# Gate-and-up products: one matmul over both activation parts, with GpSimd folding the halves

## The reference

```
def swiglu(x, w_gu, w_down):
    g, u = jnp.split(x @ w_gu, 2, axis=-1)     # x 512x1024, w_gu 1024x5632
    return (jax.nn.silu(g) * u) @ w_down
```

## Time and profile before

| | us |
|---|---|
| median of 3 runs (lowest, highest) | 2150.84 (2150.32, 2151.48) |
| the profiled execution's own time | 2148.99 |
| its span | 2147.3 |
| TensorE busy | 2129.5 |
| VectorE busy | 1612.1 |
| ScalarE busy | 1195.5 |
| GpSimd busy | 110.4 |

### The profile page before, as it was taken

The page is one execution under the profiler, slowest core; times in us unless marked ns, Lnnn a source line. Parts: engine busy times, 40 slices in busy tenths (PEclk is TensorE's granted clock), DMA queues, the critical chain, the costliest instruction groups (busy, mean ns, idle before and its releaser), DMA issues.

```text
span 2147.3 us, 36470 instructions
## 1 busy us (share of the span) xinstructions
PE 2129.5 (99%) x13624; PEld 1916.4 (89%) x13624; DVE 1612.1 (75%) x2299; ACT 1195.5 (56%) x1943; POOL 110.4 (5%) x104
## 2 busy tenths in 40 slices
PE   9999999999999999999999999999999999999998
PEld 8999988775888899998899998898889889999987
DVE  8888886798565688889688889855367566888894
ACT  6555654476564565556465556455456446555562
POOL 0000000576000000000000000000000000000000
PEclk9999999999999999999999999999999999999999
DMA  4333432221352223333413333322323422333332
GB/s 158 107 98 115 139 115 68 79 77 52 137 168 79 79 99 107 98 117 118 157 62 105 107 114 131 127 84 94 104 79 118 157 79 72 105 106 100 129 107 97
DMA packets 74498, 227.80 MB, mean 106 GB/s; under 512 B 8177, under 2 KB 22641, under 8 KB 74402
## 3 DMA queue, kind: packets, MB, share of 16 engines
q1 hardware_dynamic: 69936, 214.98, 30.3%
q10 hardware_dynamic: 4466, 11.53, 1.5%
HBM read 224.39 MB, written 2.10 MB: 105 GB/s over the span
## 4 chain that ended last, share of the span: by engine, by line
PE 93%; DVE 4%; ACT 1%; POOL 1%; issue 1%; DMA 0%; DVEq 0%; POOLq 0%; ACTq 0%
PE ps L2411 13%; PE ps L2413 13%; PE ps L2412 13%; PE ps L2457 7%; PE ps L2458 7%; PE ps L2459 7%; PE ps L511 6%; PE ps L512 6%; PE ps L513 6%; PE ps L2583 4%; PE ps L2584 4%; PE ps L2585 4%; PE ps L2347 1%; DVE e_sc L2071 0%; DVE e_max L2070 0%
## 5 line engine op out<-in xcount | busy, mean ns | idle before, releaser
L2411 PE MATMUL ps<-t_hi,w_hi 128*128 128x256 f32 x1280 | 362.3, 283 | 0.0
L2412 PE MATMUL ps<-t_lo,w_hi 128*128 128x256 f32 x1280 | 362.2, 283 | 0.0
L2413 PE MATMUL ps<-t_hi,w_lo 128*128 128x256 f32 x1280 | 362.2, 283 | 0.0
L449 DVE TENSOR_TENSOR w_lo<-w_raw,w_hi 128x1024 fp32r<-128x1024 f32 x180 | 222.6, 1240 | 172.2 <-ACT w_hi L444 171.5
L444 ACT ACTIVATE w_hi<-w_raw 128x1024 fp32r<-128x1024 f32 x186 | 195.9, 1056 | 169.5 <-DMA w_raw<-in_wstream 117.3
L1684 DVE TENSOR_TENSOR w_lo<-f,w_hi 128x1024 fp32r<-128x1024 f32 x152 | 186.2, 1225 | 123.9 <-ACT w_hi L956 123.9
L2411 PE MATMUL ps<-x_hi,w_hi 128*128 128x256 f32 x960 | 271.7, 283 | 0.0
L2412 PE MATMUL ps<-x_lo,w_hi 128*128 128x256 f32 x960 | 271.7, 283 | 0.0
L2413 PE MATMUL ps<-x_hi,w_lo 128*128 128x256 f32 x960 | 271.7, 283 | 0.0
L511 PE MATMUL ps<-x_hi,w_hi 128*128 128x256 f32 (+1 forms) x736 | 250.3, 340 | 1.9 <-DVE x_lo L1561 1.1
L512 PE MATMUL ps<-x_lo,w_hi 128*128 128x256 f32 (+1 forms) x736 | 245.9, 334 | 0.0
(11 more groups left out here) (390 smaller groups left out, 4642.6 us busy)
## 6 DMA issues: line engine op xcount, KB each, us to landing
w_raw<-in_wstream SPq DMA_DIRECT2D x286, 512.0 KB, 3.5
w_raw_odd<-in_wstream SPq DMA_DIRECT2D x80, 512.0 KB, 3.5
x_raw<-in_wstream SPq DMA_DIRECT2D x28, 512.0 KB, 5.8
gain_bc<-in_wstream SPq DMA_DIRECT2D x8, 512.0 KB, 7.0
tmp<-in_post_gains ACTq DMA_DIRECT2D x8, 512.0 KB, 3.6
gain_bc<-in_gains ACTq DMA_DIRECT2D x7, 512.0 KB, 4.7
h<-in_x SPq DMA_DIRECT2D x4, 512.0 KB, 6.1
c_mem<-in_mem ACTq DMA_DIRECT2D x2, 1024.0 KB, 5.4
```

Of the source, the lines that this page charges most:

```text
L449: nc.vector.tensor_tensor(wl, raw(v), wh.bitcast(f32), ALU.subtract).then_inc(w_ready, 1)
L2411: nc.tensor.matmul(dst, wh[:, at], xh[:, b, :], start=first, stop=False, skip_group_check=True)
L2412: nc.tensor.matmul(dst, wh[:, at], xl[:, b, :], start=False, stop=False, skip_group_check=True)
L2413: last = nc.tensor.matmul(dst, wl[:, at], xh[:, b, :], start=False, stop=final, skip_group_check=True)
```

## The change

In `product` one matmul of 512 columns takes the upper weights by both activation parts (upper and lower, now neighbours in one tile `x_both` or `t_both`), into the two halves of a bank; a matmul of 256 columns adds the lower weights by the upper activations to the first half. What a bank holds is then the sum of its two halves, and the copies and gate sums work on 512 columns:

```
-                    xh, xl = moving(MOVING[n])
+                    both = moving(MOVING[n])
                     for b in range(KT // 2):
                         at = slice(b * P, (b + 1) * P)
-                        first, final = start and b == 0, b == KT // 2 - 1
-                        nc.tensor.matmul(dst, wh[:, at], xh[:, b, :], start=first, stop=False, skip_group_check=True)
-                        nc.tensor.matmul(dst, wh[:, at], xl[:, b, :], start=False, stop=False, skip_group_check=True)
-                        last = nc.tensor.matmul(dst, wl[:, at], xh[:, b, :], start=False, stop=final,
-                                                skip_group_check=True)
+                        nc.tensor.matmul(dst, wh[:, at], both[:, :, b, :], start=start and b == 0, stop=False,
+                                         skip_group_check=True)
+                        last = nc.tensor.matmul(dst[:, 0, :], wl[:, at], both[:, 0, b, :], start=False,
+                                                stop=b == KT // 2 - 1, skip_group_check=True)
```

ScalarE copies whole banks (K1, K2, K3, K5 are 512 wide); the silu waits for the new gate fold and stands behind `last_upper`:

```
                     else:
+                        act.wait_ge(gu_free, n0 + PLAIN + 2)
                         act.wait_ge(u_sum, pair_count(it, par, 1, s0 + 2))
-                    nc.scalar.activation(place, bank(SETS[par][src])[:, 0:HB], ACT.Copy).then_inc(kept, 1)
+                    nc.scalar.activation(place, bank(SETS[par][src]), ACT.Copy).then_inc(kept, 1)
 def pair_silu(it, par):
-                    act.wait_ge(g_sum, pair_count(it, par, 2, 2 * s0 + 4))
+                    act.wait_ge(g_fold, pair_count(it, par, 1, s0 + 1))
...
                     sum_upper(*nxt, 1)
-                    pair_silu(it, par)
                     act.wait_ge(w_free, pair_count(it, par, 2, u0 + 4))
                     last_upper(1 - par)
+                    pair_silu(it, par)
```

GpSimd takes over `up_second` (512 columns, then its own fold), folds the gate and writes the last lower weights:

```
+                def up_second(it, par):
+                    pool.wait_ge(kept, pair_count(it, par, 4, 4 * s0 + 4))
+                    nc.gpsimd.tensor_tensor(K5, K5, K3, ALU.add).then_inc(u_add, 1)
+                    pool.wait_ge(u_add, pair_count(it, par, 1, s0 + 1))
+                    k5 = tmp[:, 0:1, :]
+                    nc.gpsimd.tensor_tensor(act_tile(it, par)[:, 1:2, :], k5[:, :, 0:HB], k5[:, :, HB:SEQ], ALU.add)\
+                        .then_inc(u_sum, 1)
+                def gate_fold(it, par):
+                    pool.wait_ge(g_sum, pair_count(it, par, 2, 2 * s0 + 4))
+                    nc.gpsimd.tensor_tensor(g_both, g_both, g_rest, ALU.add).then_inc(g_fold, 1)
+                def last_lower(it, par):
+                    pool.wait_ge(w_hi_ready, pair_count(it, par, 2, u0 + 2))
+                    pool.wait_ge(w_ready, pair_count(it, par, 2, u0 + 1))
+                    wh, wl = half_slots(i, 6, 1)
+                    nc.gpsimd.tensor_tensor(wl, pair_raw(par)[:, SEQ:UW], wh.bitcast(f32), ALU.subtract)\
+                        .then_inc(w_ready, 1)
+                def period(it, par, more=True):
+                    up_second(it, par)
+                    gate_fold(it, par)
+                    if more:
+                        last_lower(it + par, 1 - par)
```

VectorE loses `up_second` and `last_lower`; its gate sums are 512 wide and go to `g_parts`; the up half that lies in bank a is folded by a reduction out of PSUM, and one product of 512 columns replaces two:

```
                 def plain_lower(it, par):
                     dve.wait_ge(w_hi_ready, pair_count(it, par, 2, u0 + 1))
+                    dve.wait_ge(w_ready, pair_count(it, par, 2, u0))
...
+                    dve.wait_ge(gu_free, pair_count(it, par, 1, n0 + 2))
+                    nc.vector.tensor_tensor(g_parts[:, 0, :], bank(SETS[par][2]), K1, ALU.add).then_inc(g_sum, 1)
...
+                def up_first(it, par):
+                    dve.wait_ge(w_free, pair_count(it, par, 2, u0 + 4))
+                    b = SETS[par][0]
+                    nc.vector.tensor_reduce(act_tile(it, par)[:, 0, :], bank(b).rearrange("p (a c) -> p c a", a=2),
+                                            AX.X, ALU.add).then_inc(u_first, 1)
+                def pair_product(it, par):
+                    up_first(it, par)
+                    pair_mul(it, par)
...
+                    nc.vector.tensor_tensor(tile, tile, g_both, ALU.mult).then_inc(gu_free, 1)
```

More of the change, by code:

```diff
@@ L105, in trunk @@
         with ExitStack() as early:
-            x_raw = [early.enter_context(nc.sbuf_tensor("x_raw0", [P, KT, SEQ], f32))]
-        x_hi = sb("x_hi", [P, KT, SEQ], f32r)
+            x_raw = [early.enter_context(nc.sbuf_tensor(f"x_raw{n}", [P, KT, SEQ], f32)) for n in range(2)]
         with ExitStack() as early:
+            early.enter_context(nc.sbuf_tensor("x_upper", [P, KT, SEQ], f32r))
             w_late_x = early.enter_context(nc.sbuf_tensor("w_late_x", [P, 2, UW], f32r))
-        with ExitStack() as early:
-            x_raw += [early.enter_context(nc.sbuf_tensor("x_raw1", [P, KT, SEQ], f32))]
-        x_lo = sb("x_lo", [P, KT, SEQ], f32r)
+        x_both = sb("x_both", [P, 2, KT, SEQ], f32r)
+        x_hi, x_lo = x_both[:, 0, :, :], x_both[:, 1, :, :]
         w_raw = sb("w_raw", [P, 2, UW])
@@ L129, in part_sb @@
                 return own.enter_context(nc.sbuf_tensor(name, shape, dt))
-            part_sb("act_first", [P, 2, SEQ])
-            t_hi = part_sb("t_hi", [P, 4, KT // 2, SEQ // 2], f32r)
-            t_lo = part_sb("t_lo", [P, 4, KT // 2, SEQ // 2], f32r)
+            g_parts = part_sb("g_parts", [P, 2, SEQ])
+            t_both = part_sb("t_both", [P, 2, 4, KT // 2, SEQ // 2], f32r)
+            t_hi, t_lo = t_both[:, 0, :, :, :], t_both[:, 1, :, :, :]
             w_raw_odd = part_sb("w_raw_odd", [P, 2, UW])
@@ L247, in trunk @@
         g_sum = sem("g_sum")
+        g_fold = sem("g_fold")
+        u_add = sem("u_add")
+        u_first = sem("u_first")
         u_sum = sem("u_sum")
@@ L459, in moving @@
             if n >= T1:
-                return t_hi[:, n - T1, :, :], t_lo[:, n - T1, :, :]
+                return t_both[:, :, n - T1, :, :]
             blocks = slice(0, KT // 2) if n == B11 else slice(KT // 2, KT)
             tokens = slice(HB, SEQ) if n == B22 else slice(0, HB)
-            return x_hi[:, blocks, tokens], x_lo[:, blocks, tokens]
+            return x_both[:, :, blocks, tokens]
         def half_slots(i, first, n):
@@ L503, in pair_in, with act_tile @@
             return it * 16 + (RAW_COUNT[u] - PLAIN // 2) * 16
-        g_both, u_second = tmp[:, 0, :], tmp[:, 1, 0:HB]
-        K1, K2, K5, K3 = (tmp[:, 2 + n // 2, n % 2 * HB:(n % 2 + 1) * HB] for n in range(4))
+        halves_of_g = g_parts[:, :, :].rearrange("p t (a b) -> p t a b", a=2)
+        g_both, g_rest = halves_of_g[:, :, 0, :], halves_of_g[:, :, 1, :]
+        K5, K3, K1, K2 = (tmp[:, n, :] for n in range(4))
+        def act_tile(it, par):
+            if isinstance(it, int):
+                return act_raw[:, 2 * it + par:2 * it + par + 1, :].rearrange("p o (a b) -> p (o a) b", a=2)
+            return act_raw[:, bass.ds(2 * it + par, 1), :].rearrange("p o (a b) -> p (o a) b", a=2)
         SEVENS = [nffn[i] * SEVEN - PLAIN for i in range(NP)]
@@ L766, in even, with ffn @@
                 poly(3)
+            def ffn(i):
+                s0, u0 = SEVENS[i], U[i, "gate_up"]
+                def up_second(it, par):
[19 more added lines that the diff above has]
+                        last_lower(it + par, 1 - par)
+                with pool.Fori(PLAIN // 2, FT // 2 - 1) as it:
+                    period(it, 0)
+                    period(it, 1)
+                period(FT // 2 - 1, 0)
+                period(FT // 2 - 1, 1, False)
             def gla(i):
@@ L783, in _ @@
                     pool.wait_ge(h_ready, TT * i)
-                if parts[i][0] == "even":
+                if parts[i][0] == "ffn":
+                    ffn(i)
+                elif parts[i][0] == "even":
                     even(i)
@@ L1695, in gate_first @@
                     dve.wait_ge(w_free, pair_count(it, par, 2, u0 + 3))
-                    nc.vector.tensor_tensor(g_both[:, 0:HB], bank(SETS[par][2])[:, 0:HB], K1, ALU.add).then_inc(g_sum, 1)
+                    dve.wait_ge(gu_free, pair_count(it, par, 1, n0 + 2))
+                    nc.vector.tensor_tensor(g_parts[:, 0, :], bank(SETS[par][2]), K1, ALU.add).then_inc(g_sum, 1)
                 def gate_second(it, par):
                     dve.wait_ge(prod, pair_count(it, par, 5, 5 * s0 + 5))
[L1700 to L1705, removed]
+                    nc.vector.tensor_tensor(g_parts[:, 1, :], bank(SETS[par][1]), K2, ALU.add).then_inc(g_sum, 1)
+                def up_first(it, par):
[6 more added lines that the diff above has]
+                    pair_mul(it, par)
                 def pair_mul(it, par):
@@ L1709, in pair_mul @@
                     dve.wait_ge(u_sum, pair_count(it, par, 1, s0 + 3))
[L1710 to L1718, removed]
+                    dve.wait_ge(u_first, pair_count(it, par, 1, s0 + 1))
+                    tile = act_tile(it, par)
+                    nc.vector.tensor_tensor(tile, tile, g_both, ALU.mult).then_inc(gu_free, 1)
                 def period(it, par, front):
@@ L1728, in period @@
```

(15 more changed lines are left out.)

## The result

Forecast: 2243 us, within 2165 to 2280, slower. Measured: the changed kernel takes 2274.02 us (median of 4 runs, 2273.10 to 2275.48), the kernel before 2150.74 (4 runs beside them, 2150.32 to 2151.48). The ratio is 1.0574, with a 95% interval of 1.0561 to 1.0586: 5.7% slower. The profiled execution took 2273.49 us, its span is 2271.8.

The account below looks back on a forecast made before the run. It took a chain through ScalarE, GpSimd and VectorE to bound the kernel: 9.7 + 19 x 11.24 us per FFN against 201.6, +23.1 x 4 = +92 on 2149.0, plus 1.8 for the runs' median: 2243 us, range 2165 to 2280.

Parts of the forecast that it names:

- The order that decides: In each pair, copy K3, GpSimd's up operations, gate fold, silu, K1 in turn: TensorE waits 1.5 us before product three.
- K1: ScalarE's copy out of PSUM for the next pair, made after this pair's silu; product three waits for it; end at 7.02.
- hand-overs at the port: GpSimd and VectorE SBUF reads exclude each other; whoever comes second waits; three such hand-overs in the chain of a pair.
- 0.15 us of overlap: Time by which a held SBUF operation overlaps the one before; without it the chain is 0.45 us longer, the total 34.
- What TensorE gains: Gate-and-up products: a block of three matmuls becomes two, 0.347 instead of 0.360 us; 29.9 us gained in all.
- both port cases: The forecast, with SBUF reads held as in the rows (chance 0.62), and the rival of half the port cost (0.15).
- No cover lost: Rival: GpSimd's and VectorE's fp32 operations pass each other at the port, chain 5.5 us, total 2121 us; chance 0.09.
- The port costs half: Rival: GpSimd needs 30% less or passes the second sum_lower; period 10.3 us, total 2172 us; chance 0.15.
- Longer GpSimd work: Rival: GpSimd's half-row folds cost 10% more or the small one 1.29 us; period 11.7, total 2277 us; chance 0.12.
- The wide matmul brings nothing: Rival: the moving operand's two halves cost what they save; 2256 us, inside the forecast's own range, no separate chance given.
- load of the shared reads: Per pair, VectorE's two-SBUF-input operations 6.0 us plus GpSimd's 4.0 make 10.0, over the 9.71 that TensorE allows.
- K3: ScalarE's copy out of PSUM after product five, forecast to end at 0.88 us; GpSimd's up sum waits for it.

Follow-up runs that it names:

- TensorE's part alone: The kernel before with only the matmuls changed, copies and gate sums still 256 wide, GpSimd idle: 2135.74 us, ratio 0.9928.
- `sum_lower` out of PSUM: The changed kernel with VectorE's two sum_lower subtractions taking their first operand from a PSUM bank instead of SBUF: 2164.64 us, ratio 1.0061 to the kernel before.

## Why the prediction was right, and what it mis-sized
**The order that decides: right, in place and size.** Counted from the start of product six (114.93), the ends of the steps in the pair above against the prediction's, in us:

| end of | predicted | measured |
|---|---|---|
| GpSimd up sum | 2.87 | 2.83 |
| gate_second | 2.41 | 2.30 |
| second sum_lower | 3.99 | 3.94 |
| half fold | 4.6 | 4.53 |
| gate fold | 5.85 | 5.78 |
| silu | 6.50 | 6.44 |
| K1 | 7.02 | 6.93 |
| start of product three | 7.06 | 6.98 |

Over 68 middle pairs the median start of product three is 7.04. So the hand-overs at the port, read from three overlaps of the earlier trace rows, hold for the new operations as well. The 0.15 us of overlap also hold: the second `sum_lower` ends at 118.87, the half fold 0.59 later, where one alone takes 0.74. The signs that it named came: 76 waits before product three, 105 us (forecast about 100); GpSimd's up sum at 1850 ns, well above 1.29 (`sum_lower`, at 1255 against 1.22, was held in the first period of an FFN alone, 2.32 us there); ScalarE waiting for the gate fold in every pair; GpSimd busy 584 us.

**What TensorE gains: the term that was mis-sized.** The prediction took the wide step from down's 0.227, among matmuls of one width. Here it is 0.234 to 0.237 and a block 0.3537 us: 28 x 80 x 0.0063 = 14 us instead of 30, as TensorE's part alone measured (15). In the stalled loop only products three to five count. They take 4.34 us (median; 114.93 - 110.58 = 4.35 above) instead of 4.16: 12 x 0.007 = 0.08 from the blocks, and 0.10 because the first wide matmul after each wait takes 0.34 us to the next start. That is why the period, 11.36 over the middle pairs, exceeds 11.24, though the chain itself was not longer than forecast.

**The stalls at the ends: the first too small.** The prediction gave the first stall of an FFN the size of the others. It is 2.15 to 2.5 us: there GpSimd's up sum comes before the first `sum_lower`, VectorE and `gate_second` slip behind it, and the gate fold meets the second `sum_lower` (2.18 us in the third FFN, 1.29 in the pair above). The last, foreseen at +1.4 for the forming of block one, is 2.5 to 2.6, the others' 1.25 and 1.3 more.

**Not foreseen: half clock.** After six of the eight long stalls the granted clock stands at half (1.2 GHz, the lower of its two levels) for 3.4 us, and some 1.5 us are lost each time: the first period takes 13.84 us in the third FFN, where the clock fell, and 12.31 in the second, where it didn't. The third FFN's first stall ends at 1185.23; windows of 2 us, with the busy time of the five engines (matmul, weight load, VectorE, ScalarE, GpSimd), the granted clock and DMA:
```profile
1183.00:1185.00 2.00, 0.08 (x1) 0.00 (x0) 0.61 (x2) 0.94 (x2) 2.00 (x2) 1.00 0.02 4
1185.00:1187.00 2.00, 1.77 (x6) 1.47 (x7) 1.97 (x3) 1.13 (x2) 0.26 (x1) 0.62 0.40 80
1187.00:1189.00 2.00, 2.00 (x9) 1.71 (x8) 2.00 (x4) 0.60 (x1) 0.00 (x0) 0.53 0.46 182
1189.00:1191.00 2.00, 2.00 (x14) 1.72 (x13) 1.00 (x1) 1.03 (x2) 0.00 (x0) 1.00 0.05 6
```

**The sum again.** Per FFN 9.9 + 19 x 11.36 + 1.3 (last) + 1.1 (first: 1.6 in the first FFN, 0.95 in the others) = 228.1, and 6 x 1.5 / 4 = 2.3 of half clock: 230.4. The four spans, from the first matmul's start to the last one's, are 229.6, 229.3, 231.3 and 231.1, against 224.7 forecast and 201.5 before: +115 us in all. The waits at down for lower weights (6.6 us), which the prediction's sum didn't have, come on top: 122 of the 123 measured.
Most of the 31 us between 2243 and 2274 is named by this: some 9 us of longer periods, 4 of first stalls, 9 of half clock and 7 at down. All of it goes one way, and the result lies outside the forecast's own range, 2220 to 2262. It is the wide range, set to take in both port cases, that holds it.

**The rivals.** *No cover lost* was 2121 us, and is refuted by GpSimd's own durations. *The port costs half* falls with the period of 11.36 where it said 10.3. *Longer GpSimd work*, at 2277, is nearer to the measured 2274 than the forecast is, so the time alone would have spoken for it. The trace speaks against it: the period isn't 11.7, the half fold takes 741 ns when it isn't held (`sum_lower` out of PSUM), and the gate fold in the middle of an FFN 1.29 us. *The wide matmul brings nothing* is half true: 15 of the 30 us are there. The load of the shared reads, 10.0 us by the prediction against a TensorE pair of 9.9, would alone hold TensorE up by about 0.1 us a pair. That is argued, not measured: `sum_lower` out of PSUM took away load and hand-overs at once.

## What to carry to other kernels
Before moving work to an idle engine, add up what it will share: here GpSimd was free and its 4.6 us fitted into 9.9, but its SBUF reads and VectorE's two-input SBUF operations together came to 10 us of one port. Then follow the chain from the producer that comes late (K3) to the buffer that the bounding engine needs (K1), with each hand-over at its held duration; a gain of 0.0063 us in each of 28 blocks, 0.18 us a pair, can't pay for a wait of 1.4 us a pair. A matmul's step read in another stage is a guess for this one: 0.227 us in down became 0.234 to 0.237 here, and halved the gain. TensorE's part of a change can be timed by itself first.

## What was not expected of the hardware
- A 512-column matmul followed by one of 256 columns takes 0.234 to 0.237 us to the next start, against 0.227 in the down projection. With alternating widths it is neither the pieces of the t operand nor the half that is written next; with four in a row it is still 0.234 from one to the next.
- The first wide matmul after a wait of TensorE takes 0.34 us to the next start, 0.10 more than the others.
- In the changed kernel eight idle times of TensorE of 2.15 to 2.6 us were followed, in six cases, by 3.4 us at half the granted clock; the 68 of 1.16 to 1.33 us in the same products were not.
- With VectorE's operand in PSUM, GpSimd's two-input fp32 operations take 741 ns for 256 columns and 1380 for 512; held by VectorE's SBUF reads 1552 and 1850.
